# Attention scores over the full height of the array, with zero-padded copies of the keys, in an encoder layer on one core

## The reference

```
D_MODEL, SEQ, ATT_HEADS, ATT_KV_HEADS, ATT_HEAD_DIM = 1024, 512, 8, 2, 64
WINDOW, ATT_BLOCK, HG_HEADS, HG_DIM, D_FF = 128, 128, 4, 128, 2816

def windowed_gqa_sink(q, k, v, sink):            # one block of 128 queries against up to 384 keys
    s = jnp.einsum('bqhgd,bkhd->bhgqk', qn, kn).astype(jnp.float32) * scale
    s = jnp.where(mn, s, NEG_INF)
    m = jnp.maximum(jnp.max(s, axis=-1, keepdims=True), sink_f)
    p = jnp.exp(s - m)
    p = p / (jnp.sum(p, axis=-1, keepdims=True) + jnp.exp(sink_f - m))
    return jnp.einsum('bhgqk,bkhd->bqhgd', p.astype(vn.dtype), vn)

x = x + 0.5 * rmsnorm(swiglu(rmsnorm(x, ...)), ...)
q, k, v, hq, hf_fwd, hf_bwd, hi, hg = split(rmsnorm(x, ...) @ w_in)
att = rmsnorm(windowed_gqa_sink(rope(q), rope(k), v, sink), attn_out_norm)
o = rmsnorm(hgrn2(forward) + hgrn2(backward), hg_out_norm) * silu(hg)
x = x + rmsnorm(concatenate([att, o]) @ w_out, ...)
x = x + 0.5 * rmsnorm(swiglu(rmsnorm(x, ...)), ...)
```

## Time and profile before

| | |
|---|---|
| median of 3 runs | 1064.55 us (1064.37 to 1065.12) |
| the profiled execution | 1064.92 us, of which the span is 1063.1 us |
| PE busy | 1046.3 us, 98% of the span |
| PE weight loads busy | 866.8 us, 82% |
| DVE, ACT, POOL busy | 425.2, 363.4, 450.5 us (40%, 34%, 42%) |
| mixer's beats with attention (500 to 641 us): L1092 | 32 matmuls, 64 records |

### The profile page before, as it was taken

The page is one execution under the profiler, slowest core; times in us unless marked ns, Lnnn a source line. Parts: engine busy times, 40 slices in busy tenths (PEclk is TensorE's granted clock), DMA queues, the critical chain, the costliest instruction groups (busy, mean ns, idle before and its releaser), DMA issues.

```text
span 1063.1 us, 13360 instructions
## 1 busy us (share of the span) xinstructions
PE 1046.3 (98%) x5075; PEld 866.8 (82%) x5075; DVE 425.2 (40%) x621; ACT 363.4 (34%) x540; POOL 450.5 (42%) x299
## 2 busy tenths in 40 slices
PE   6999999999999999999999999999999999999997
PEld 5988888888888878888777878898888888888886
DVE  4443443434001160365757576644434343420103
ACT  6322222222112264513656575542222222221211
POOL 3444444444444246863324134135444444444440
PEclk9999999999999999999999999999999999999999
DMA  6333333323433243332010114024323333333212
GB/s 221 99 99 99 99 99 89 99 89 99 138 99 99 80 137 100 80 99 60 21 40 21 41 40 139 10 74 136 99 86 98 92 99 99 99 99 119 98 41 80
DMA packets 136300, 96.00 MB, mean 90 GB/s; under 512 B 11442, under 2 KB 120387, under 8 KB 136260
## 3 DMA queue, kind: packets, MB, share of 16 engines
q1 hardware_dynamic: 136080, 95.43, 29.8%
q10 hardware_dynamic: 180, 0.02, 0.0%
HBM read 93.34 MB, written 2.10 MB: 90 GB/s over the span
## 4 chain that ended last, share of the span: by engine, by line
PE 94%; DVE 3%; ACT 1%; issue 1%; DMA 1%; ACTq 0%; DVEq 0%
PE ps L832 19%; PE ps L834 18%; PE ps L833 18%; PE ps L841 9%; PE ps L840 9%; PE ps L839 9%; PE ps L998 2%; PE ps L1092 2%; PE ps L1032 1%; PE ps L1115 1%; PE ps L857 1%; PE ps L1102 1%; DVE YB L1286 1%; ACT SQX L514 1%; DMA vec_rows<-hgrn_out_norm 1%
## 5 line engine op out<-in xcount | busy, mean ns | idle before, releaser
L413 POOL TENSOR_TENSOR WL<-raw,WH 128x1024 fp32r<-128x1024 f32 x132 | 317.1, 2404 | 424.3 <-ACT WH L492 424.3
L832 PE MATMUL ps<-XH,WH 128*128 128x512 f32 (+1 forms) x944 | 360.8, 382 | 0.1
L834 PE MATMUL ps<-XH,WL 128*128 128x512 f32 (+1 forms) x944 | 354.7, 376 | 0.0
L833 PE MATMUL ps<-XL,WH 128*128 128x512 f32 (+1 forms) x944 | 354.5, 376 | 0.0
L492 ACT ACTIVATE WH<-raw 128x1024 fp32r<-128x1024 f32 x162 | 171.0, 1056 | 324.9 <-PE ps L834 172.5
L832 PEld LDWEIGHTS ps<-XH,WH 128*128 128x128 f32 x944 | 178.4, 189 | 44.4 <-issue 13.7
L834 PEld LDWEIGHTS ps<-XH,WL 128*128 128x128 f32 x944 | 178.2, 189 | 32.5
L833 PEld LDWEIGHTS ps<-XL,WH 128*128 128x128 f32 x944 | 178.4, 189 | 31.9 <-issue 1.2
L839 PE MATMUL ps<-WH,hh 128*128 128x512 f32 x352 | 137.1, 389 | 0.0
L841 PE MATMUL ps<-WL,hh 128*128 128x512 f32 x352 | 137.0, 389 | 0.0
L430 POOL TENSOR_TENSOR WL<-raw,WH 128x256 fp32r<-128x256 f32 x120 | 95.2, 828 | 98.5 <-ACT WH L492 98.3
(11 more groups left out here) (163 smaller groups left out, 881.3 us busy)
## 6 DMA issues: line engine op xcount, KB each, us to landing
raw<-ffn_w_gate SPq DMA_DIRECT2D x44, 512.0 KB, 3.7
raw<-ffn_w_up SPq DMA_DIRECT2D x44, 512.0 KB, 3.7
raw<-ffn_w_down SPq DMA_DIRECT2D x44, 512.0 KB, 3.7
raw<-w_in SPq DMA_DIRECT2D x22, 512.0 KB, 3.7
raw<-w_out SPq DMA_DIRECT2D x8, 512.0 KB, 3.3
X<-x SPq DMA_DIRECT2D x4, 512.0 KB, 6.5
raw<-w_in SPq DMA_DIRECT2D x8, 256.0 KB, 3.2
out<-X SPq DMA_DIRECT2D x8, 256.0 KB, 2.0
```

Of the source, the lines that this page charges most:

```text
L413: pool.tensor_tensor(low, raw[:, s, :], high.bitcast(fp32), ALU.subtract).then_inc(lo_done, 1)
L832: nc.tensor.matmul(dst, WH[:, s, w], xh, start=first, stop=False)
L833: nc.tensor.matmul(dst, WH[:, s, w], xl, start=False, stop=False)
L834: return nc.tensor.matmul(dst, WL[:, s, w], xh, start=False, stop=last)
```

## The change

The matmul L1092 takes all 128 rows of `qT` (both heads of pair j) and, for its other operand, one of two key tiles: `kT`, whose rows 64 to 127 are set to zero, for kv = 0, and the new tile `kT1`, whose rows 0 to 63 are zero, for kv = 1. The other head's rows of the query meet zeros. For the key unit `turned` replaces one addition over 128 partitions by two over 64 partitions each, and adds two memsets of 64 x 512 floats, of which the last signals `rope_done`. The query units are as before. `kT1` is placed after all other tiles of its region, so no other tile moves. Nothing changes in number or order on PE, ACT, POOL or SP.

```diff
--- before.py
+++ after.py
@@ -161,12 +161,12 @@
                 return [region.enter_context(nc.sbuf_tensor(n, s, d)) for n, s, d in wanted]
 
         hid = [place((f"hh{f}", [P, KF, TOK], f32r), (f"hl{f}", [P, KF, TOK], f32r)) for f in (1, 2)]
-        V, W, Fg, OS, qT, kT, VA, AG, GT, Qh, KS, SD, SX, KM, masks, rope, swap, band = place(
+        V, W, Fg, OS, qT, kT, VA, AG, GT, Qh, KS, SD, SX, KM, masks, rope, swap, band, kT1 = place(
             ("V", [P, TT, TOK], fp32), ("W", [P, 2, 4, TOK], fp32), ("Fg", [P, 2, 2, TOK], fp32),
             ("OS", [P, TT, TOK], fp32), ("qT", [P, G, TOK], fp32), ("kT", [P, TOK], fp32), ("VA", [P, TT, P], fp32),
             ("AG", [P, TOK], fp32), ("GT", [P, 2, TOK], fp32), ("Qh", [P, 2, TOK], fp32), ("KS", [P, 2, TOK], fp32),
             ("SD", [P, 2, TOK], fp32), ("SX", [P, 3, TOK], fp32), ("KM", [P, 2, TOK], fp32), ("masks", [P, 7, TOK], u8),
-            ("rope", [P, 2, TOK], fp32), ("swap", [P, P], fp32), ("band", [P, 3 * P], fp32))
+            ("rope", [P, 2, TOK], fp32), ("swap", [P, P], fp32), ("band", [P, 3 * P], fp32), ("kT1", [P, TOK], fp32))
 
 
         K = 256
@@ -176,6 +176,7 @@
             ("ELb", [P, 2, SLOT], f32r))
         _, S = place(("to_S", [P, 83 * K + K // 2], fp32), ("S", [P, SRING, 3 * P], fp32))
         EH, EL = ([x[:, b, :] for x in pair for b in range(2)] for pair in ((EHa, EHb), (ELa, ELb)))
+        KZ = (kT, kT1)
         PT = TMP
         AT = [AT01[:, 0, :], AT01[:, 1, :], GT[:, 0, :], GT[:, 1, :]]
         GTREE = (GT, SQ)
@@ -1082,14 +1083,13 @@
                 b, n = divmod(i, HQ)
                 k0, nk = keys_at(b)
                 j, kv = n // 2, n % 2
-                r = slice(kv * DH, (kv + 1) * DH)
                 if i:
                     pe.wait_ge(s_max, i)
                 else:
                     pe.wait_ge(proj_taken, len(COPIED))
                 if i < HQ:
                     pe.wait_ge(rope_done, 2 + j)
-                nc.tensor.matmul(ps[2][:, 0:nk * P], qT[r, j, chunk(b)], kT[r, k0 * P:(k0 + nk) * P],
+                nc.tensor.matmul(ps[2][:, 0:nk * P], qT[:, j, chunk(b)], KZ[kv][:, k0 * P:(k0 + nk) * P],
                                  start=True, stop=True).then_inc(s_ready, 1)
 
             def att_turn(i):
@@ -1454,7 +1454,14 @@
                 step(nc.vector.tensor_tensor(SQX[:, 0, :], TMP[:, j % 2, :], rope[:, 0, :], ALU.mult))
                 dve.wait_ge(rot_ready, TURNED.index(n) + 1)
                 step(nc.vector.tensor_tensor(to, ps[6][:, :], rope[:, 1, :], ALU.mult))
-                nc.vector.tensor_tensor(to, to, SQX[:, 0, :], ALU.add).then_inc(rope_done, 1)
+                if MIXU[n][0] == "q":
+                    nc.vector.tensor_tensor(to, to, SQX[:, 0, :], ALU.add).then_inc(rope_done, 1)
+                    return
+                low, high = slice(0, DH), slice(DH, P)
+                step(nc.vector.tensor_tensor(kT1[high, :], kT[high, :], SQX[high, 0, :], ALU.add))
+                nc.vector.tensor_tensor(kT[low, :], kT[low, :], SQX[low, 0, :], ALU.add)
+                nc.vector.memset(kT1[low, :], 0.0)
+                nc.vector.memset(kT[high, :], 0.0).then_inc(rope_done, 1)
 
             def out_gate(n):
```

## The result

The changed kernel takes 1059.07 us in the median of four runs (1057.48 to 1061.12), the kernel before 1064.74 beside it. The ratio is 0.9947 with a 95% interval of 0.9935 to 0.996: 5.7 us faster. The prediction was 1055.7 in a range of 1052.5 to 1059.5, so the sign and the range held and the size was 3.4 us too large. It lies 0.4 us inside the upper end of the range; the median of all fourteen executions that were measured in the end, 1060.1, lies outside it. The profiled execution, at 1061.12 us, is the slowest of the four.

The account below looks back on a forecast made before the run. TensorE, busy 98% of the span, was taken as the bound: 14.4 us saved less losses left 9.85, less 0.8 for VectorE's stall, so -9.05 from 1064.92 gave 1055.9; stated 1055.7, range 1052.5 to 1059.5.

Parts of the forecast that it names:

- rival 1: At L1092, only the drain on the way back is due to height; gain shrinks by a third, 1059.1 us; chance 0.10.
- rival 2: In attention beats, ScalarE and VectorE take over more often; about 3 us of gain goes, 1058.7 us; chance 0.13.
- TensorE drains on both sides of a 64-row matmul: At L1092, the array runs empty going from 128 rows to 64 and again on the way back; excess 0.45 us.
- rival 3: At L1092's load, the gap stays at full height, leaving only VectorE's added time; 1065.7 us; chance 0.05.
- rival 4: Along VectorE and ScalarE chains, half the 4.55 us of losses returns and L1042 does not stall; 1052.8 us; chance 0.10.
- 0.45 us an item: On TensorE, each of the 32 L1092 matmuls gets 0.45 us shorter, 14.4 us if TensorE bounds everywhere.
- Where savings are lost: Attention items where savings become waits: 0 to 3 (1.7 us), 5 to 7 (0.6), 18 (0.45), 27 to 30 (1.8).
- VectorE's four instructions: Ahead of copy L1376, they take 2.7 us, 1.7 more than before; 0.9 is hidden, so L1042 waits 0.8 us.
- The rule on weight loads: Skill rule: loads overlap matmuls only in different row groups, so L1092 would gain nothing on TensorE; left out of the sum.

Follow-up runs that it names:

- late_split_act: late_split with, on ScalarE, beat 14's head-unit sigmoids moved behind beat 15's KM and beat 41's high part behind that beat's exp; 1055.08 us, ratio 0.9909.
- vector_only: The changed kernel with its four VectorE instructions and two key tiles, but L1092 over 64 rows again; 1066.22 us, ratio 1.0011.
- rows128_only: The kernel before with L1092 over all 128 rows, both heads' keys in place, no second key tile and no zeros; 1058.18 us, ratio 0.9934.
- late_split: The changed kernel with the second key tile and the zeros written at beat 10, where VectorE is idle; 1058.23 us, ratio 0.9934.
- filled: The changed kernel with fp32 identity matmuls keeping TensorE busy in its two longest waits; median 1059.22 us.
- nine_short: The changed kernel with L1092 over 64 rows for items 0 to 3, 18 and 27 to 30, 128 rows for the other 23; 1058.67 us.
- late_split_filled: late_split with the fillers of filled in TensorE's two longest waits; 1057.07 us.

## Why the prediction was right, and where its size was off

The number by itself decides little. 1059.07 is also what rival 1 (1059.1) and rival 2 (1058.7) gave, and that it fell inside the range is partly luck: the sum left out a cost (the clock, below), and with ten more executions the median is 0.6 us beyond the range. What the runs bear out is the mechanism.

The lead of a kernel over the kernel before can be read at the start of L1092 of every item, out of the two timelines. What each stretch gave, forecast against two executions of the changed kernel and the last experiment:

| from L1092 of item .. to .. | forecast | after, no fall | after, two falls | late_split_act |
|---|---|---|---|---|
| 0 to 4 | 0.10 | 0.21 | -0.67 | 2.42 |
| 4 to 5 | 0.45 | 0.35 | -0.33 | -0.97 |
| 5 to 8 | 0.75 | 0.14 | 0.12 | 0.07 |
| 8 to 18 | 4.50 | 3.92 | 3.96 | 3.92 |
| 18 to 19 | 0 | -0.21 | -0.21 | -0.21 |
| 19 to 27 | 3.60 | 3.26 | 3.26 | 3.28 |
| 27 to 31 | 0 | -0.22 | -1.08 | 0.75 |
| 31 to the output projection | 0.45 | 0.11 | -0.40 | 0.10 |
| sum | 9.85 | 7.56 | 4.65 | 9.36 |

- *TensorE drains on both sides of a 64-row matmul.* Right, and shown three ways: by the loads, by the 128-row run without zeros, and by the 0.424 us of the added matmuls. Rival 1, that only the way back is due to the height, falls: the load ahead of L1092 is early now. With it falls rival 3, and of rival 4 (more comes through) nothing was seen.
- *0.45 us an item.* Mis-sized: 0.39 to 0.41, in the mean of the two long stretches of the table. The 1.12 us that I took for four L998 and an L832 came from a beat in which an L834 of 512 columns stands ahead of the L998; in attention beats it is L1115, with 64 columns, and L999 takes 522.29 - 521.35 = 0.94 us there instead of 0.89. Over 23 items about 1.2 us.
- *Where savings are lost.* All places were right: items 0 to 3, 18 and 27 to 30 gave nothing, as the run with nine short items shows. Sizes: items 5 to 7 gave 0.14 and not 0.75, because two waits fall there, for the exp of item 6 (0.4 us) and for VectorE's L1421 (0.3), and I had counted one. By the starts they cost more than that, 0.59 us (L835 to L1102: 0.82 instead of 0.23) and 0.47 (L1115 to L1010: 0.86 instead of 0.39), and 3 x 0.4 - 1.06 = 0.14. Item 18 and the last stretch gave some 0.2 and 0.3 less. This is rival 2 in small.
- *VectorE's four instructions.* Taken as 2.7 us, measured 3.44, which is past the high end of 3.36, so the wait of L1042 is 1.3 us and not 0.8; that is within its ends (0 to 1.4). The slow value of the earlier trace rows held for both additions (1.09 and 1.11), and a memset over 64 partitions takes 0.48. The wait passes through in full (vector_only).
- *Missing from the sum: the clock.* I counted each new wait by its length. Two of them reached 1.9 to 2.1 us, and in some executions TensorE's clock was at 1.2 GHz behind them, at 1.6 us for the first and 1.4 for the second. That makes the difference between 7.56 and 4.65 us in the table. The changed kernel varies from 1057.5 to 1061.5 us, once to 1064.8; but the kernel before, in the same session, varied from 1064.0 to 1068.3, so the wider spread is not all new. That falls become frequent with these two waits is shown by counting executions with a mean clock below 0.999: 8 of 14 of the changed kernel, 4 of 5 of rows128_only and 3 of 5 of late_split, which have both waits; none of 14 of the three kernels in which the waits are filled, short, or gone (filled, nine_short, late_split_act). It is not these waits alone: with waits of 0.7 us there the kernel before has 2 of 21 and 0 of 9, vector_only 1 of 11, and late_split_filled, where they are filled, 1 of 5, all at 0.998. What decides it in one execution stays open.
- *The rule on weight loads.* The sentence of the Trainium skill ("TensorE: Matmul & The Clock Gate", Part 3) stands in the section "The mechanism", and not in the one that the prediction names. The rows after still go against it: a full-height load starts under a full-height matmul.

Taken together: 9.85 - 1.2 (size of an item) - 1.1 (the rest of the table) - 1.3 for L1042 makes 6.3 us without a fall; the six executions at 0.999 gave 1064.8 - 1057.9 = 6.9, which agrees within the 1 us by which single executions differ ahead of item 0. Eight of the fourteen executions have one fall or more, at some 1.5 us each, and so the two medians over all executions are 4.6 and 5.7 us.

## What to carry to other kernels

A matmul over part of the rows between full-height ones costs two drains, here 0.42 us together; fill the rows with zeros, or put half-height matmuls for the two halves side by side, where the second is nearly free. Before you shorten the bound engine, list its waits and ask what each will be afterwards: savings ahead of a wait only lengthen it. And keep TensorE's waits short, or fill them: here 2 us of idling cost some 1.5 us more through the clock, in about every second execution, and moving two things on ScalarE was worth as much as half of the change itself.

## What was not expected of the hardware

- Behind a wait of 1.9 to 2.1 us TensorE's granted clock fell to 1.2 GHz for 3.3 and 3.4 us of full work, in some executions; behind the waits of 0.7 to 1.3 us from 450 to 655 us no trace shows it. Of four traces with a wait of 2.0 to 2.1 us for KM, three show 2.4 GHz throughout behind it.
- Two 64-row matmuls over the two halves of the rows, into two banks, take 0.872 us where one takes 0.857, no difference that one execution each can tell.
- An addition over 64 partitions is no shorter for it: two additions 64x512, beside GpSimd, took 1.09 and 1.11 us, as the one 128x512 had (1.09). A memset of 64x512 took 0.48 us and, in late_split, a copy of 64x512 within SBUF 0.42; neither has a full-height counterpart here.
